# The second block's four attentions as one run of 64 steps, with masks and key bias added in PSUM

## The chip, the cores and the metric

One core of one Trainium2 chip runs the whole kernel. The metric is the device time of one execution in microseconds (us); the times are medians over several executions. Everything is float32; large products of the projections are made as three products of parts (a high part and a remainder, type fp32r).

## What is computed

Two blocks of a network over 1024 tokens of 1024 channels. The change lies in the second block, which projects its input and runs four mixers side by side, of which two are causal attentions with 4 heads of 64 channels each:

```
# forgetting attention, c = cumsum(log_sigmoid(f + bias)) per head
logits = q @ k.T * 64**-0.5 + c[query] - c[key]
logits = where(key <= query, logits, -inf);  out = softmax(logits) @ v
# stick-breaking attention
z = q @ k.T * 64**-0.5
log_rest = where(key < query, log_sigmoid(-z), 0)
between = reversed_cumsum(log_rest) - log_rest
out = where(key < query, exp(log_sigmoid(z) + between), 0) @ v
```

c[query] is the same for a whole row and falls out of the softmax; the kernel leaves it out. The mixers' outputs are gated by a sigmoid of a projection of 4096 channels, then merged, projected and followed by a feed-forward layer.

## The kernel before, in words

Engines run their own streams of instructions and wait for each other through semaphores. A part of the program between two barriers is a phase (`core.phase`, L96); at its end all engines meet and the semaphores are cleared. The second block (`second_block`, L1142) projects to a buffer in device memory (`proj2_kept`) and then runs `s5_branch`, `rwkv_branch` and `attention_branches` (L1252) in that order; `gated_branches` (L1175) follows.

**Gate tiles.** The gates' projection is 32 tiles of 128 channels, cut into 16 pieces each (two halves of 512 tokens by 8 slices of channels; a piece is three matmuls of 512 columns, L519). `GateTiles` (L494) hands pieces out: each of the three mixers calls `gates.tensor(pe, n)` wherever TensorE would wait. A half sums in one PSUM bank (bank 7, or 6 and 7 by turns where `gates.two` is set); VectorE scales it into `gate_stage` (`gates.vector`, L546), SyncE stores it and loads the weight tile after next (`gates.sync`, L557, L559, L149), and GpSimd splits the next weight tile into two parts (`gates.gpsimd`, L156, L158). Each queue is in order.

**Attentions.** After a small load (`load`, L601), a first phase makes one gate tile (16 pieces) and, for the forget bias, two 4x1024 sums and a scan on VectorE, three passes on ScalarE, and then eight products against a selector that spread the four rows over 128 partitions (L1288), which ScalarE copies out as `key_bias` (L1316). Then come four pairs of heads, forgetting first, then stick-breaking. For each pair one phase loads queries, keys and values (L1325, 1.5 MB), transposes the values on TensorE (L1332) and copies them out on ScalarE (L1339), and another runs 16 steps, one for each head and block of 128 queries. Step (n, j) has j+1 blocks of 128 keys. `causal_products` (L1349) writes TensorE's order out by hand: iteration i makes the scores of step i into one of two pairs of PSUM banks (L1362), the output of step i-3 (L1380) and the transposes of the weights of step i-2 (L1370). In the stick pairs alone 3 and 5 gate pieces by turns lie between these, 64 per pair.

A forgetting step (`forgetting_pair`, L1415) has VectorE scale the scores out of PSUM and add the key bias (L1440), add the mask on the diagonal block (L1444), take the row's largest value and negate it (L1445, L1446); ScalarE takes the exponential and its sum (L1471), VectorE the reciprocal (L1452) and the scaling (L1453). A stick step (`stick_pair`, L1475) has VectorE scale the scores out of PSUM (L1543), ScalarE make Abs, Exp and Ln (L1510 to L1512), VectorE a sum (L1527), a mask on the diagonal block (L1528), a scan (L1530), a subtraction (L1532) and another mask (L1533), and ScalarE an exponential (L1516). In both, the transposed weights are copied out of PSUM by ScalarE (L1403, helper `save_transposed`) and the output by VectorE (L1411, helper `save_output`). A score of step i+2 waits only until VectorE has copied the score of step i out of PSUM.

## Time and profile before

| | |
|---|---|
| median of 3 runs | 3998.53 us (3997.77 to 3999.42) |
| profiled execution | 3993.96 us, its span 3992.2 us |
| granted TensorE clock, mean | 0.943 |
| busy | TensorE 89%, VectorE 42%, ScalarE 19%, GpSimd 22% |
| attention stage | about 2412 to 2845 us of the span |

The profile is one execution. Windows of the span give, for each engine, the time in which it was busy; the granted clock is 1.00 at 2.4 GHz and 0.50 at 1.2 GHz. Starts in the order of time are us from the span's start. TensorE's matmuls overlap, so the distance between two starts says more than a duration. A float32 matmul appears as two records, a transpose as one.

### The profile page before, as it was taken

The page shows a single profiled execution, that of the slowest core. Times are in us where ns is not written, and L with a number is a line of the kernel's source. Part 1 is how long each engine was busy: PE and PEld are TensorE (multiplying, and loading weights), DVE is VectorE, ACT ScalarE, POOL GpSimd, SP SyncE. Part 2 cuts the span into 40 slices and gives each one's busy share as a digit, 9 for nine tenths or more (in the row PEclk, how much of TensorE's full clock was granted, in tenths as well). Part 3 has the DMA queues.
Part 4 walks back from the last instruction along what each step waited for, and adds up shares of the span by engine and source line. Part 5 has one row for each costly group of instructions (what it writes and reads, how often), then busy time and mean ns, then how long its engine had stood idle before and what let it go on. Part 6 is the DMA issues. An engine that isn't in the chain of part 4 may idle for free. (4 is left out here: it accounts for less than half of the span.)

```text
span 3992.2 us, 42576 instructions
## 1 busy us (share of the span) xinstructions
PE 3556.5 (89%) x17914; PEld 2923.2 (73%) x17914; DVE 1674.5 (42%) x2127; ACT 767.8 (19%) x1065; POOL 893.2 (22%) x513
## 2 busy tenths in 40 slices
PE   7988999998898989897877988788898799999996
PEld 6976878897687978776757975455446578888884
DVE  3225662322566251255456554656563321212134
ACT  2112331111333110000112212344320210101012
POOL 2340003234000323331124310011002133334331
PEclk9999999999999999998989997788999899999998
DMA  2120001112000133311220011011350111111111
GB/s 91 43 83 16 7 1 43 43 43 86 7 7 1 43 112 110 115 48 43 78 76 24 1 48 43 16 53 48 121 174 27 50 41 52 48 48 48 48 53 48
DMA packets 68666, 208.52 MB, mean 52 GB/s; under 512 B 10564, under 2 KB 16324, under 8 KB 68332
## 3 DMA queue, kind: packets, MB, share of 16 engines
q1 hardware_dynamic: 64012, 189.53, 14.7%
q10 hardware_dynamic: 4464, 16.25, 1.0%
q8 instruction: 143, 2.34, 0.2%
q14 instruction: 47, 0.39, 0.0%
HBM read 164.80 MB, written 40.37 MB: 51 GB/s over the span
## 5 line engine op out<-in xcount | busy, mean ns | idle before, releaser
L156 POOL CAST w_hi<-w_raw 128x1024 fp32r<-128x1024 f32 x187 | 206.7, 1105 | 2773.2 <-POOLq L104 1400.4
L158 POOL TENSOR_TENSOR w_lo<-w_raw,w_hi 128x1024 fp32r<-128x1024 f32 x187 | 511.2, 2734 | 15.0
L167 PE MATMUL psum<-h_hi,w_hi 128*128 128x512 f32 x1008 | 315.4, 394 | 35.0 <-DVE h_lo L188 29.1
L167 PE MATMUL psum<-h_lo,w_hi 128*128 128x512 f32 x1008 | 311.8, 391 | 0.0
L167 PE MATMUL psum<-h_hi,w_lo 128*128 128x512 f32 x1008 | 311.7, 390 | 0.0
L519 PE MATMUL psum<-h_hi,w_hi 128*128 128x512 f32 x512 | 217.1, 424 | 47.9 <-PEq L104 24.9
L167 PEld LDWEIGHTS psum<-h_hi,w_hi 128*128 128x128 f32 x1008 | 190.0, 189 | 79.8 <-issue 40.2
L167 PEld LDWEIGHTS psum<-h_lo,w_hi 128*128 128x128 f32 x1008 | 190.3, 189 | 39.8
L167 PEld LDWEIGHTS psum<-h_hi,w_lo 128*128 128x128 f32 x1008 | 190.1, 189 | 39.7
L519 PE MATMUL psum<-h_lo,w_hi 128*128 128x512 f32 x512 | 205.2, 401 | 0.0
L519 PE MATMUL psum<-h_hi,w_lo 128*128 128x512 f32 x512 | 204.8, 400 | 0.0
L167 PE MATMUL psum<-hn_hi,w_hi 128*128 128x348 f32 x864 | 186.6, 324 | 2.3 <-DVE hn_lo L185 2.3
L167 PE MATMUL psum<-hn_hi,w_lo 128*128 128x348 f32 x864 | 184.0, 321 | 0.0
L167 PE MATMUL psum<-hn_lo,w_hi 128*128 128x348 f32 x864 | 183.7, 321 | 0.0
L519 PEld LDWEIGHTS psum<-h_hi,w_hi 128*128 128x128 f32 x512 | 99.5, 194 | 91.2 <-issue 50.6
L167 PE MATMUL psum<-ff_lo,w_hi 128*128 128x512 f32 x512 | 157.6, 389 | 0.0
L167 PE MATMUL psum<-ff_hi,w_hi 128*128 128x512 f32 x512 | 157.6, 389 | 0.0
L167 PE MATMUL psum<-ff_hi,w_lo 128*128 128x512 f32 x512 | 157.6, 389 | 0.0
L2765 DVE TENSOR_TENSOR h_again<-psum,h_again 128x1024 f32<-128x1024 f32 x32 | 39.2, 1225 | 272.8 <-PE psum L167 272.8
L167 PEld LDWEIGHTS psum<-hn_hi,w_hi 128*128 128x128 f32 x864 | 145.8, 188 | 5.5 <-issue 3.8
L167 PEld LDWEIGHTS psum<-hn_lo,w_hi 128*128 128x128 f32 x864 | 145.7, 188 | 0.0
L167 PEld LDWEIGHTS psum<-hn_hi,w_lo 128*128 128x128 f32 x864 | 145.6, 188 | 0.0
(411 smaller groups left out, 6660.7 us busy)
## 6 DMA issues: line engine op xcount, KB each, us to landing
w_raw<-in_w_mlp SPq DMA_DIRECT2D x64, 512.0 KB, 3.6
w_raw<-in_w_in SPq DMA_DIRECT2D x36, 512.0 KB, 3.6
w_raw<-in_w_gates SPq DMA_DIRECT2D x32, 512.0 KB, 3.8
gates_kept<-gate_stage SPq DMA_DIRECT2D x64, 256.0 KB, 2.1
gates<-gates_kept SPq DMA_DIRECT2D x32, 512.0 KB, 3.6
w_raw<-in_w_out SPq DMA_DIRECT2D x24, 512.0 KB, 3.6
w_raw<-in_w_branches_in SPq DMA_DIRECT2D x23, 512.0 KB, 3.6
proj_kept<-stage ACTq DMA_DIRECT2D x23, 512.0 KB, 2.6
```

Source lines behind the costliest of these rows:

```text
L156: self.core.nc.gpsimd.tensor_copy(self.hi[:, g % 2], self.raw[:, g % 2]).then_inc(self.hi_done, 1)
L158: self.core.nc.gpsimd.tensor_tensor(self.lo[:, g % 2], self.raw[:, g % 2], self.hi[:, g % 2].bitcast(F32), ALU.subtract) \
L167: last = nc.tensor.matmul(acc[:, c, :], w[:, g % 2, k, :], x(k)[:, c * ch:(c + 1) * ch], start=(k == 0 and part == 0), stop=(k == kt - 1 a ...
L519: last = nc.tensor.matmul(self.core.psum[:, self.bank(x // KT), :], one[:, g % 2, k, :], other(k)[:, c * CH2:(c + 1) * CH2], start=(k == 0 ...
L2765: nc.vector.tensor_tensor(halves(h(m)), acc[g % 2], halves(h(m)), ALU.add) \
```

## The change

All four pairs go into one phase of 64 steps, stick-breaking pairs first. Queries are scaled by 1/8 on GpSimd when they are loaded, and queries and keys of a head stand at partitions 0 to 63, in two buffers by turns, so that a pair is loaded while an earlier one is worked on (values have one load buffer; they are transposed 8 steps ahead). The mask of the diagonal block is added by a product of the identity with the mask that sums onto the scores in PSUM. The key bias is a 65th row: ones beside the queries, the scan of the negated log-sigmoid beside the keys. ScalarE and VectorE read the scores in PSUM, and a score of step i+2 waits until the last reader of step i is done: the subtraction in a stick step (`stick_free`), the exponential in a forgetting step (`fox_exp`). Two gate pieces lie in each step, before and after the output; the first tile stands in front of the run. The largest value is taken with its sign turned in one operation. `attention_branches` takes the place of the seven functions; their removed bodies are those printed above, and the selector goes from `second_tables`:

```diff
--- before.py
+++ after.py
 def attention_branches(core, io, gates, masks, vecs, ybr):
...
-def bank_pair(core, s, n):
...
-def causal_products(core, gates, pe, qk, v, prob, probT, masks, score_free, scores_done, prob_ready,
...
-def save_transposed(core, act, i, j, probT, probT_done, probT_saved, out_done):
...
-def save_output(core, eng, i, n, j, pair, ybr, branch, out_done, out_saved):
...
-def forgetting_pair(core, gates, pair, qk, v, logits, soft, probT, key_bias, one_row, small, masks, ybr, branch):
...
-def stick_pair(core, gates, pair, qk, v, logits, soft, probT, key_bias, one_row, small, masks, ybr, branch):
...
+    gates.two = False
+    q = core.sb("queries", [P, 2, 2, T2])
+    k = core.sb("keys", [P, 2, 2, T2])
+    v_in = core.sb("values", [P, T2])
+    v = core.sb("v2", [P, 2, NQ2, P])
+    prob = core.sb("logits", [P, 3, T2])
+    rest = core.sb("rest", [P, T2])
+    small = core.sb("small2", [P, 3, 2], align=32)
+    fbias = core.sb("fbias", [HEADS2, 1], align=32)
+    nmx, total, inv = (small[:, i, :] for i in range(3))
+    f, e = gate[:, 0, :], gate[:, 1, :]
+    heads = [(1, BR_STICK, 0), (1, BR_STICK, 1), (0, BR_FOX, 0), (0, BR_FOX, 1)]
+    steps = [(p, n, j) for p in range(4) for n in range(2) for j in range(NQ2)]
+    count = len(steps)
+    def stick(i):
+        return 0 <= i < count // 2
+    def fox(i):
+        return count // 2 <= i < count
+    def width(i):
+        return (steps[i][2] + 1) * P
+    def scores(i):
+        return core.psum[:, 2 * (i % 2):2 * (i % 2) + 2, :].rearrange("p a n -> p (a n)")[:, 0:width(i)]
+    with core.phase("at_f_in", "at_q0", "at_q1", "at_k0", "at_k1", "at_v_in", "at_bias_in", "at_ones", "at_row",
+                    "at_scaled", "at_vT", "at_v", "at_f", "at_f_act", "at_scores", "sb_abs", "sb_ln", "sb_arg",
+                    "sb_free", "sb_prob", "fx_bias", "fx_exp", "fx_inv", "fx_prob", "at_T", "at_Tsaved", "at_out",
+                    "at_saved") as \
+            (block, f_in, q_in0, q_in1, k_in0, k_in1, v_in_done, bias_in, ones_set, row_set, q_scaled, vT_done,
+             v_saved, f_dve, f_act, scores_done, abs_step, ln_ready, arg_step, stick_free, stick_prob, fox_bias,
+             fox_exp, fox_inv, fox_prob, probT_done, probT_saved, out_done, out_saved):
+        q_in, k_in = (q_in0, q_in1), (k_in0, k_in1)
+            def load_pair(p):
+                kind, _, pair = heads[p]
+                m = P_ATT + 6 * kind + 3 * pair
+                if p >= 2:
+                    sp.wait_ge(out_done, 16 * (p - 1))
+                if p >= 1:
+                    sp.wait_ge(vT_done, p)
+                sp.dma_start(v_in[:], io["proj2"][m + 2]).then_inc(v_in_done, 16)
+                for n in range(2):
+                    sp.dma_start(q[0:64, p % 2, n, :], io["proj2"][m, 64 * n:64 * n + 64]).then_inc(q_in[p % 2], 16)
+                    sp.dma_start(k[0:64, p % 2, n, :], io["proj2"][m + 1, 64 * n:64 * n + 64]) \
+                        .then_inc(k_in[p % 2], 16)
+            load_pair(0)
+            sp.dma_start(f, io["proj2"][P_FORGET, 0:HEADS2, :]).then_inc(f_in, 16)
+            sp.dma_start(fbias[:], io["forget_bias"]).then_inc(f_in, 16)
+            load_pair(1)
+            sp.wait_ge(f_dve, 4)
+            for p in range(2):
+                for n in range(2):
+                    hd = 2 * p + n
+                    sp.dma_start(k[64:65, p, n, :], gate[hd:hd + 1, 0, :]).then_inc(bias_in, 16)
+            for p in range(4):
+                gates.sync(sp, 2)
+                if p < 2:
+                    load_pair(p + 2)
+            def scale_queries(p):
+                pool.wait_ge(q_in[p % 2], 32 * (p // 2 + 1))
+                nc.gpsimd.tensor_scalar(q[0:64, p % 2], q[0:64, p % 2], ATT_SCALE, None, ALU.mult) \
+                    .then_inc(q_scaled, 1)
+            nc.gpsimd.memset(one_row[:], 1.0).then_inc(ones_set, 1)
+            scale_queries(0)
+            pool.wait_ge(ones_set, 1)
+            pool.wait_ge(q_scaled, 1)
+            nc.gpsimd.memset(q[64:65], 1.0).then_inc(row_set, 1)
+            pool.wait_ge(row_set, 1)
+            scale_queries(1)
+            for p in range(4):
+                gates.gpsimd(pool, 2)
+                if p < 2:
+                    scale_queries(p + 2)
+            def value_transposes(p):
+                pe.wait_ge(v_in_done, 16 * (p + 1))
+                for t in range(NQ2):
+                    last = nc.tensor.transpose(core.psum[:, 4 + t // 4, (t % 4) * P:(t % 4 + 1) * P],
+                                               v_in[:, t * P:(t + 1) * P], masks[:, M_IDENT, :])
+                last.then_inc(vT_done, 1)
+            def score(i):
+                p, n, j = steps[i]
+                rows = slice(0, 64 if stick(i) else 65)
+                if n == 0 and j == 0:
+                    pe.wait_ge(k_in[p % 2], 32 * (p // 2 + 1))
+                    pe.wait_ge(q_scaled, p + 1)
+                    if p == 2:
+                        pe.wait_ge(row_set, 1)
+                        pe.wait_ge(bias_in, 64)
+                if stick(i - 2):
+                    pe.wait_ge(stick_free, i - 1)
+                if fox(i - 2):
+                    pe.wait_ge(fox_exp, i - 1 - count // 2)
+                for c in range((width(i) + CH2 - 1) // CH2):
+                    w = min(CH2, width(i) - c * CH2)
+                    diagonal = c == j // 4
+                    nc.tensor.matmul(core.psum[:, 2 * (i % 2) + c, 0:w], q[rows, p % 2, n, j * P:(j + 1) * P],
+                                     k[rows, p % 2, n, c * CH2:c * CH2 + w], start=True, stop=not diagonal)
+                    if diagonal:
+                        nc.tensor.matmul(core.psum[:, 2 * (i % 2) + c, w - P:w], masks[:, M_IDENT, :],
+                                         masks[:, M_NEG_FROM if stick(i) else M_NEG_AFTER, :],
+                                         start=False, stop=True).then_inc(scores_done, 1)
+            def transposes(i):
+                if stick(i):
+                    pe.wait_ge(stick_prob, i + 1)
+                else:
+                    pe.wait_ge(fox_prob, i + 1 - count // 2)
+                if i >= 1:
+                    pe.wait_ge(probT_saved, i)
+                for t in range(steps[i][2] + 1):
+                    last = nc.tensor.transpose(core.psum[:, 4 + t // 4, (t % 4) * P:(t % 4 + 1) * P],
+                                               prob[:, i % 3, t * P:(t + 1) * P], masks[:, M_IDENT, :])
+                last.then_inc(probT_done, 1)
+            def output(i):
+                p, n, j = steps[i]
+                pe.wait_ge(probT_saved, i + 1)
+                if i >= 1:
+                    pe.wait_ge(out_saved, i)
+                for t in range(j + 1):
+                    last = nc.tensor.matmul(core.psum[64 * n:64 * n + 64, 6, 0:P], v[:, p % 2, t, 64 * n:64 * n + 64],
+                                            probT[:, t, :], start=(t == 0), stop=(t == j))
+                last.then_inc(out_done, 1)
+            gates.tensor(pe, KT)
+            value_transposes(0)
+            gates.tensor(pe, KT)
+            pe.wait_ge(v_saved, 1)
+            for i in range(count + 3):
+                if i < count:
+                    score(i)
+                    gates.tensor(pe, 1)
+                    output(i - 3)
+                if i % 16 == 8 and i < count - 16:
+                    pe.wait_ge(probT_saved, i - 2)
+                    value_transposes(i // 16 + 1)
+                if i < count:
+                    gates.tensor(pe, 1)
+                if i % 16 == 8 and i < count - 16:
+                    pe.wait_ge(v_saved, i // 16 + 2)
+                if 2 <= i < count + 2:
+                    transposes(i - 2)
+            def save_values(p):
+                act.wait_ge(vT_done, p + 1)
+                nc.scalar.activation(v[:, p % 2].rearrange("p (a t) n -> p a (t n)", a=2), core.psum[:, 4:6, :],
+                                     ACT.Copy).then_inc(v_saved, 1)
+            save_values(0)
+            for i in range(count + 2):
+                if i % 16 == 8 and i < count - 16:
+                    save_values(i // 16 + 1)
+                    act.wait_ge(probT_done, i - 1)
+                    if i >= 3:
+                        act.wait_ge(out_done, i - 2)
+                    nc.scalar.activation(probT[:].rearrange("p t n -> p (t n)")[:, 0:width(i - 2)],
+                                         core.psum[:, 4:6, :].rearrange("p a n -> p (a n)")[:, 0:width(i - 2)],
+                                         ACT.Copy).then_inc(probT_saved, 1)
+                if stick(i):
+                    sp = soft[:, i % 2, 0:width(i)]
+                    act.wait_ge(scores_done, i + 1)
+                        act.wait_ge(stick_free, i - 1)
+                    step(nc.scalar.activation(sp, scores(i), ACT.Abs))
+                if fox(i):
+                    act.wait_ge(fox_bias, i + 1 - count // 2)
+                    act.wait_ge(probT_done, i - 2)
+                    nc.scalar.activation(prob[:, i % 3, 0:width(i)], scores(i), ACT.Exp, bias=nmx[:, i % 2:i % 2 + 1],
+                                         accum_out=total[:, i % 2:i % 2 + 1]).then_inc(fox_exp, 1)
+                if stick(i - 1):
+                    lg = prob[:, (i - 1) % 3, 0:width(i - 1)]
+                    act.wait_ge(stick_free, i)
+                    nc.scalar.activation(lg, lg, ACT.Exp).then_inc(stick_prob, 1)
+                if i == 0:
+                    act.wait_ge(f_dve, 1)
+                    step(nc.scalar.activation(e, f, ACT.Abs))
+                    step(nc.scalar.activation(e, e, ACT.Exp, scale=-1.0))
+                    nc.scalar.activation(e, e, ACT.Ln, bias=1.0).then_inc(f_act, 1)
+            link = chain(dve, arg_step)
+            gates.vector(dve)
+            dve.wait_ge(f_in, 32)
+            nc.vector.tensor_scalar(f, f, fbias[:, 0:1], None, ALU.add).then_inc(f_dve, 1)
+            gates.vector(dve)
+            dve.wait_ge(ones_set, 1)
+            for i in range(count + 3):
+                if i % 4 == 0 and 0 < i <= count:
+                if fox(i):
+                    b = slice(i % 2, i % 2 + 1)
+                    if i - 2 >= count // 2:
+                        dve.wait_ge(fox_exp, i - 1 - count // 2)
+                    nc.vector.reduce_max(nmx[:, b], scores(i), AX, negate=True).then_inc(fox_bias, 1)
+                if stick(i - 1):
+                    w = width(i - 1)
+                    lg, sp = prob[:, (i - 1) % 3, 0:w], soft[:, (i - 1) % 2, 0:w]
+                    dve.wait_ge(ln_ready, i)
+                    link(nc.vector.scalar_tensor_tensor(out=sp, in0=scores(i - 1), scalar=0.0, in1=sp,
+                                                        op0=ALU.max, op1=ALU.add))
+                    if i >= 2:
+                        dve.wait_ge(stick_free, i - 1)
+                    link(nc.vector.tensor_tensor_scan(rest[:, 0:w][:, ::-1], one_row[:, 0:w], sp[:, ::-1], 0.0,
+                                                      ALU.mult, ALU.add))
+                    if i >= 4:
+                        dve.wait_ge(probT_done, i - 3)
+                    nc.vector.tensor_tensor(lg, scores(i - 1), rest[:, 0:w], ALU.subtract).then_inc(stick_free, 1)
+                if fox(i - 1):
+                    b, w = slice((i - 1) % 2, (i - 1) % 2 + 1), width(i - 1)
+                    done = i - count // 2
+                    dve.wait_ge(fox_exp, done)
+                    if done >= 2:
+                        dve.wait_ge(fox_prob, done - 1)
+                    nc.vector.reciprocal(inv[:, b], total[:, b]).then_inc(fox_inv, 1)
+                    dve.wait_ge(fox_inv, done)
+                    nc.vector.tensor_scalar(prob[:, (i - 1) % 3, 0:w], prob[:, (i - 1) % 3, 0:w], inv[:, b], None,
+                                            ALU.mult).then_inc(fox_prob, 1)
+                if i == 1:
+                    dve.wait_ge(f_act, 1)
+                    nc.vector.tensor_scalar(f, f, 0.0, None, ALU.min).then_inc(f_dve, 1)
+                    dve.wait_ge(f_dve, 2)
+                    nc.vector.tensor_tensor(e, e, f, ALU.subtract).then_inc(f_dve, 1)
+                    dve.wait_ge(f_dve, 3)
+                    nc.vector.tensor_tensor_scan(f, one_row[0:HEADS2, :], e, 0.0, ALU.mult, ALU.add).then_inc(f_dve, 1)
+                    p, n, j = steps[i - 3]
+                    _, branch, pair = heads[p]
+                    rows = slice(64 * n, 64 * n + 64)
+                    dve.wait_ge(out_done, i - 2)
+                    nc.vector.tensor_copy(ybr[rows, pair + branch, j * P:(j + 1) * P],
+                                          core.psum[rows, 6, 0:P]).then_inc(out_saved, 1)
+    return {k: np.ascontiguousarray(v.astype(f32)) for k, v in dict(masks=m, s5_select=sel).items()}
```

## Rows read from the trace of the kernel before

**Rows 1.** Windows by stage: stretch, its us, busy of each engine, granted clock, DMA share, GB/s
```profile
2414.00:2442.00 28.00, 22.37 (x64) 13.65 (x64) 6.89 (x7) 9.84 (x9) 3.81 (x2) 0.80 0.14 45
2442.00:2452.00 10.00, 1.97 (x8) 1.57 (x8) 0.00 (x0) 1.02 (x1) 0.00 (x0) 0.50 0.45 158
2452.00:2475.00 23.00, 21.95 (x53) 11.48 (x54) 15.25 (x40) 7.37 (x17) 0.00 (x0) 0.50 0.00 0
2475.00:2520.00 45.00, 36.45 (x209) 25.13 (x208) 29.18 (x72) 17.51 (x32) 0.00 (x0) 0.96 0.00 1
...
2617.00:2726.00 109.00, 97.86 (x456) 67.13 (x456) 78.32 (x120) 52.74 (x81) 13.77 (x8) 0.95 0.12 39
```

**Rows 2.** Waits, attention stage: engine, line, releaser: us in total, times, longest
```profile
PE psum L1332 <- DMA qkv<-proj_kept: 32.3, 4, 8.8
```

**Rows 3.** Order of time, VectorE, end of the attentions: start, us, instruction, idle before
```profile
2844.68 0.29 DVE L1411 COPY branches<-psum 64x128 f32<-64x128 f32 x1 [3.80 <-PE psum L1380]
```

**Rows 4.** Order of time, TensorE: start of the phase; then iteration 6 of a stick pair
```profile
2417.40 0.77 PE L519 MATMUL psum<-h_hi,w_hi 128*128 128x512 f32 x1 [5.21 <-PEq L104]
...
2646.27 1.77 PE L1362 MATMUL psum<-qkv 64*128 64x512 f32 x4
2647.97 1.09 PE L1380 MATMUL psum<-probT,v 128*64 128x128 f32 x8
2648.98 0.50 PE L519 MATMUL psum<-h_hi,w_hi 128*128 128x512 f32 x1
...
2649.78 0.71 PE L1370 MATMUL psum<-masks,logits 128*128 128x128 f32 x5
2650.25 0.48 PE L519 MATMUL psum<-h_hi,w_hi 128*128 128x512 f32 x1
```

**Rows 5.** The same stretch: a ScalarE copy; a VectorE save and TensorE behind it
```profile
2650.53 0.70 ACT L1403 ACTIVATE probT<-psum 128x640 f32<-128x640 f32 x1 [1.14 <-PE psum L1370]
...
2659.82 0.28 DVE L1411 COPY branches<-psum 64x128 f32<-64x128 f32 x1
...
2660.24 1.50 PE L1380 MATMUL psum<-probT,v 128*64 128x128 f32 x12 [0.28 <-DVE branches L1411]
```

**Rows 6.** Groups by form, attention stage: line, engine, shapes, count; busy, mean ns; idle
```profile
L1530 DVE TENSOR_TENSOR_SCAN key_bias<-one_row,soft 128x1024 f32<-128x1024 f32 x4 | 9.2, 2292 | 0.1
...
L1527 DVE SCALAR_TENSOR_TENSOR soft<-logits,soft 128x512 f32<-128x512 f32 x4 | 8.6, 2139 | 0.0
L1403 ACT ACTIVATE probT<-psum 128x1024 f32<-128x1024 f32 x8 | 8.2, 1024 | 26.4 <-PE psum L1370 26.4
...
L1532 DVE TENSOR_TENSOR logits<-logits,key_bias 128x1024 f32<-128x1024 f32 x4 | 4.9, 1225 | 0.1
...
L1440 DVE SCALAR_TENSOR_TENSOR logits<-psum,key_bias 128x1024 f32<-128x1024 f32 x4 | 4.9, 1225 | 4.5 <-PE psum L1362 4.4
...
L1510 ACT ACTIVATE soft<-logits 128x1024 f32<-128x1024 f32 x4 | 4.2, 1046 | 0.0
...
L1403 ACT ACTIVATE probT<-psum 128x128 f32<-128x128 f32 x8 | 2.2, 277 | 14.5 <-PE psum L1370 14.5
...
L1530 DVE TENSOR_TENSOR_SCAN key_bias<-one_row,soft 128x128 f32<-128x128 f32 x4 | 1.7, 424 | 0.1
...
L1532 DVE TENSOR_TENSOR logits<-logits,key_bias 128x128 f32<-128x128 f32 x4 | 1.2, 293 | 0.1
```

**Rows 7.** Order of time, SyncE's queue: the first load of the attention stage
```profile
2414.16 0.27 SPq L607 DMA_DIRECT2D forget<-proj_kept  x1
```

**Rows 8.** Groups by form, GpSimd, whole span; columns as in the groups above
```profile
L158 POOL TENSOR_TENSOR w_lo<-w_raw,w_hi 128x1024 fp32r<-128x1024 f32 x187 | 511.2, 2734 | 15.0
L156 POOL CAST w_hi<-w_raw 128x1024 fp32r<-128x1024 f32 x187 | 206.7, 1105 | 2773.2 <-POOLq L104 1400.4 <-PE psum L167 1041.1 <-PE psum L519 236.1
...
L1716 POOL TENSOR_SCALAR rw_raw<-rw_raw 128x1024 f32<-128x1024 f32 x2 | 6.6, 3316 | 33.9 <-DVE rw_mixed L1683 33.8
...
L2323 POOL MEMSET s_toeplitz<- 128x2048 f32 x1 | 1.8, 1812 | 0.0
```

More of the change, by code:

```diff
@@ L1260, in attention_branches @@
     one_row = core.sb("one_row", [P, T2])
-    small = core.sb("small2", [P, 4, 2])
-    sel = core.sb("head_select", [HEADS2, HEADS2, P])
-    fbias = core.sb("fbias", [HEADS2, 1])
     gate = core.sb("forget", [HEADS2, 2, T2])
-    load(core, [(gate[:, 0, :], io["proj2"][P_FORGET, 0:HEADS2, :]), (sel[:], io["head_select"]),
-                (fbias[:], io["forget_bias"])])
-    gates.two = True
-    with core.phase("f_step_act", "f_step_dve", "c_done", "c_saved") as (block, f_act, f_dve, c_done, c_saved):
+    small = core.sb("small2", [P, 3, 2], align=32)
@@ L1306, in _ @@
-        @block.scalar
-        def _(act):
-            link = chain(act, f_act)
-            act.wait_ge(f_dve, 2)
-            f, e = gate[:, 0, :], gate[:, 1, :]
-            link(nc.scalar.activation(e, f, ACT.Abs))
-            link(nc.scalar.activation(e, e, ACT.Exp, scale=-1.0))
-            link(nc.scalar.activation(e, e, ACT.Ln, bias=1.0))
-            for n in range(HEADS2):
-                act.wait_ge(c_done, n + 1)
-                nc.scalar.activation(halves(key_bias[:, n, :]), core.psum[:, 2 + 2 * (n % 2):4 + 2 * (n % 2), :],
-                                     ACT.Copy, scale=-1.0).then_inc(c_saved, 1)
@@ L1535, in _ @@
-            for i in range(len(steps) + 3):
-                if i % 2 == 0 and 0 < i <= len(steps):
+            link = chain(dve, arg_step)
[6 more added lines that the diff above has]
+                if i % 4 == 0 and 0 < i <= count:
                     gates.vector(dve)
-                if i < len(steps):
-                    w = (steps[i][1] + 1) * P
+                if fox(i):
+                    b = slice(i % 2, i % 2 + 1)
```

206 lines of the change are left out of this document (removed).

## The prediction

> **What bounds the kernel now.** I read the windows by stage first, then the waits, then TensorE's order of time inside one step, then the groups of the ScalarE and VectorE instructions. Only the stretch from 2412 to 2845 us is touched; all else is taken as unchanged. In it TensorE never sets the pace alone: the start phase takes 28 us, and before each of the four pairs comes a stretch like the one from 2442 to 2452, 10 us in which TensorE is busy for 2 [rows 1]. There it waits for the load of queries, keys and values, 32.3 us over the four pairs [rows 2]. Behind it the granted clock stays at 0.50, the 1.2 GHz level, for 23 us in the first forgetting pair, where TensorE has only attention work; at 2475 it is back [rows 1]. A stick pair, which carries 64 pieces of gate product, lasts 109 us with TensorE busy for 98 [rows 1]. The stage ends with the last save of an output at 2844.7 + 0.3 = 2845.0 [rows 3]. A gain here counts one for one, since the next stage waits for this one, and its own first load comes only then.
>
> **Costs of one step, from TensorE's order of time.** A step has b blocks of 128 keys, b = 1 to 8. Start to start: a score of 7 blocks 1.70 us, an output of 4 blocks 1.01, one gate piece 0.80, five transposes 0.47 [rows 4]. Eight against twelve output records (4 and 6 blocks) are 1.09 and 1.50 us busy, 0.21 a block [rows 4, 5]. So: score 0.23 + 0.21b, output 0.17 + 0.21b, transposes 0.094b, piece 0.79 with its change of operands.
>
> **The change, part by part.**
> - *Mask and key bias in TensorE.* Each step gains one 128x128 product against the identity: a block of 0.21 and a change of weights of 0.1, 0.31 us. Bounds 0.2 and 0.45. The 65th row of a forgetting score adds nothing to what streams: 0; if it did, at most the 0.1 of a change per score. VectorE loses the scaling copies of the stick steps, both edits of a diagonal block, and in the forgetting steps the scale-and-add, the mask and the negation. The VectorE work that goes lies under TensorE once TensorE bounds; it counts through the chain below.
> - *Gates.* 144 pieces before and after: 16 before the first step, then two in every one of the 64 steps instead of four in each of 32. TensorE's step is then P(b) = 0.23 + 0.21b + 0.31 + 2 x 0.79 + 0.17 + 0.21b + 0.094b = 2.29 + 0.514b, over b = 1 to 8 36.8 us a head.
> - *Stick steps: a new chain.* Scores are now read where they lie, so score i+2 waits until step i's subtraction has read them. In order of time: transposes of i-2 end TensorE's iteration i; ScalarE copies them out, then Abs, Exp, Ln of i; VectorE does sum, scan, subtraction; then TensorE's whole iteration i+2 can run. ScalarE's copy goes from 277 ns at one block to 1024 at eight, 0.17 + 0.107b, and a pass over the scores is 0.02 longer (1046) [rows 6]: three are 0.57 + 0.32b. The scan is 0.157 + 0.267b and a two-input pass 0.16 + 0.133b [rows 6]: together 0.48 + 0.533b. Handovers: 0.28 from the next instruction behind the transposes (2650.25) to the copy (2650.53) [rows 4, 5], 0.14 from a VectorE end at 2660.10 to TensorE at 2660.24 [rows 5], some 0.1 for the rest. L(b) = 1.74 + 0.96b. It closes over two iterations, so a step takes (L + P)/2 = 2.01 + 0.737b, or P where that is longer (b = 1 alone, 2.80). Over b = 1 to 8: 42.7 us; four heads 171 us.
> - *Forgetting steps.* Their chain is one reduction, one exponential and the copy, at eight blocks some 1.2 + 1.1 + 1.0, and the buffer is free long before iteration i+2. They go at TensorE's P: 4 x 36.8 = 147, and 4 us for waits that I can't place.
> - *Start.* The separate load goes (first issue 2414.2, TensorE from 2417.4 [rows 4, 7]): TensorE starts at about 2414.3. Eight pieces at 0.68 are 5.5, 1.5 more for the matmuls at 1.2 GHz that the first rows after a break show, value transposes 0.9, eight pieces 5.5: first score at 2428. The four products that spread the forget row and their copies are gone (12 us, TensorE until 2440). The values' load lies under the first pieces.
> - *POOL.* In front of the first tile's split now stand the ones, the scaling of 64x2048 queries, and a 4096-element row. The nearest scaling, 128x1024, took 3.3 us, the nearest fill of 2048 1.8, cast and difference of a tile 1.1 + 2.7 [rows 8]. Queries landed at 2419, scaling 2.2 (at the cast's rate) to 6.6, row 3.6, split 3.8: 2428.6 to 2432.9, wanted at 2428.8. 0 to 4 us; I take 2.
> - *Forget bias.* The three ScalarE passes and the 4x1024 scan sit in iterations 0 and 1, partly in the wait above: 1 us (0 to 6). SP waits for the scan before the next tile's load, which is two tiles early: 0. The four bias rows are needed 32 steps later: 0.
> - *Loads of the next pair.* Those of pairs 2 and 3 wait for the 16th and 32nd output, about iteration 18 and 34, and are needed at 32 and 48: hidden under 13 steps, over 50 us. Behind that wait in SP's queue stands the load of the tile after next, 0; behind POOL's scaling stands a split due at iteration 24, 0. Without that cover each would be the 10 us of now.
> - *Values.* Three times eight transposes, a ScalarE copy of 1.0 and TensorE's wait for it in the midst of the run: 2 us each, 6 (3 to 9).
> - *End.* The last copies stand between the last outputs: 4 us more than the sum of P holds.
> - *Shared access.* A VectorE pass of 512 columns that should take 0.7 took 2.1 on average where a tile's split ran beside it [rows 6]. In a run of eight tiles and three scalings I count 3 us (0 to 14).
>
> Sum: 2428 + 2 + 171 + 151 + 1 + 6 + 4 + 3 = 2766, against 2845: 79 us less. The profiled execution took 3994.0 (span 3992.2), which gives 3915; the median of the runs is 4.6 above it, so 3920.
>
> **A rule weighed.** VectorE's pass of 1024 columns out of PSUM took 1225 ns, that out of SBUF 1225 [rows 6]: reading scores in place costs nothing extra. The Trainium skill (VectorE: DVE Perf Modes, the cycle table under the TRN2 errata) gives a PSUM source 62 cycles, 65 ns, more than an SBUF source; an estimate by that page is two such reads on each of 32 chains, 4 us, half of it per closed loop, so 2 us on the sum. The trace doesn't agree with it, and the sum goes by the trace.
>
> **Rivals.**
> - *A. TensorE bounds the stick steps too* (the two-iteration chain overlaps better than I have it). For: TensorE was busy for 98 of 109 us there. Against: today the scores leave PSUM at once. 148 in place of 171: 3897.
> - *B. More waits of POOL and VectorE on the chain.* All 14 us of shared access, 4 for the split, 5 for the forget passes, 10 for the steps' irregular widths: some 28 worse, 3948.
> - *C. The clock falls (slower than before).* With scores held in PSUM TensorE pauses in every stick step at its head; if the chip answers with 1.2 GHz, P doubles. All through, stick steps gain 32 x 4.6 / 2 = 74 us and forgetting steps 147: 4141. It ends slower than before from 79/221, 36 per cent of the run at the lower level. For: 23 us at 0.50 behind one break. Against: the breaks behind which it fell were about 10 us; from 2475 to 2520 TensorE was idle for 8.5 us of 45 in short pauses and the clock was 0.96 [rows 1]. The Trainium skill (TensorE: Matmul & The Clock Gate, the second failure mode by PSUM-queue cycling) says that such short pauses make the clock oscillate; by that rule this rival holds, and this stretch of the trace does not agree.
> - *D. The run in one piece does not hide its loads* (the head of a queue waits too long). Three loads of 10 us and their restart at the low clock, some 15 each: 3965. For it speaks only that SP, POOL and TensorE all wait in order.
>
> **How the numbers follow.** Forecast 0.71 (own range 3902 to 3940), A 0.12, B 0.09, D 0.03, C 0.05, of which 0.03 slower than before. The range takes in A with the lower bounds of mask and start, and B with some of D: 3890 to 3956. What a measurement can tell from no change is about 0.2 per cent, 8 us: faster 0.95, same 0.02, slower 0.03.
>
> **What would show it.** Right: attention from its first score to its last save about 338 us, no TensorE idle over 5 us in it, granted clock 0.98 or more; stick steps of eight blocks near 7.9 us with TensorE waiting at each score for the subtraction; forgetting steps of eight blocks near 6.4 with TensorE never waiting; ScalarE's value copies with a wait of a few us three times. Wrong: a clock under 0.9 (C), stick heads of 37 us (A), TensorE idle behind a DMA at steps 16, 32 or 48 (D), gate pieces waiting for a split (B). The forecast as a whole is wrong if the stage ends less than 40 or more than 110 us earlier.

## The result, and the profile after

The changed kernel took 3930.52 us (median of four runs, 3927.46 to 3934.08) against 3998.98 for the kernel before in the same comparison (3997.77 to 4007.15): a ratio of 0.9825, interval 0.9808 to 0.9842, some 68 us faster. The profiled execution took 3927.89 us (span 3926.1), 66.1 less than that of before; the mean granted clock went from 0.943 to 0.955. The forecast was 3920 in 3890 to 3956.

The page of the changed kernel, part 1 (busy time, share of the span, instructions). VectorE does less, as the change means; TensorE's share is up by one point.

```profile
PE 3531.9 (90%) x18026; PEld 2917.6 (74%) x18026; DVE 1606.8 (41%) x1934; ACT 753.2 (19%) x1057; POOL 922.5 (23%) x519
```

The stage is read from the store ahead of it to the end of the last save of an output. Before: 2412.94 to 2844.97, 432.0 us (its end is in [rows 3]). Now the queue of SP has the store and, 1.2 us behind it, the first load; the columns are start, duration, engine, line:

```profile
2415.40 0.32 SPq L559 DMA_DIRECT2D gates_kept<-gate_stage  x1
2416.62 0.32 SPq L1308 DMA_DIRECT2D values<-proj_kept  x1
```

and VectorE's last save:

```profile
2777.55 0.29 DVE L1515 COPY branches<-psum 64x128 f32<-64x128 f32 x1 [3.81 <-PE psum L1397]
```

So the stage takes 2777.84 - 2415.40 = 362.4 us, 69.6 less. The 2.46 by which it starts later lies in code that is the same in both. In the executions below that store lies anywhere from 2408.54 to 2422.80, so **one execution's span says little to 5 us, and the experiments are read by the length of the stage** beside their medians.

The windows of the stage, where before were the gaps and the slow clock of [rows 1]: the four stick heads in turn, and the four forgetting heads with the end. Columns: length, busy time and instructions of TensorE's matmuls, its weight loads, VectorE, ScalarE, GpSimd, then the granted clock, the DMA share and GB/s.

```profile
2431.00:2477.00 46.00, 35.32 (x140) 21.76 (x141) 30.58 (x33) 22.09 (x37) 19.77 (x8) 0.85 0.13 40
2477.00:2522.00 45.00, 39.86 (x204) 26.14 (x204) 26.22 (x34) 25.93 (x42) 1.99 (x1) 1.00 0.07 24
2522.00:2572.00 50.00, 41.66 (x195) 27.20 (x196) 29.97 (x37) 24.12 (x39) 10.17 (x4) 0.93 0.19 53
2572.00:2621.00 49.00, 42.66 (x207) 28.25 (x205) 25.60 (x33) 26.92 (x43) 3.20 (x2) 0.93 0.07 22
2621.00:2778.00 157.00, 149.84 (x849) 109.56 (x849) 68.98 (x145) 51.84 (x104) 19.17 (x9) 1.00 0.13 39
```

The forgetting heads are bound by TensorE, busy for 150 of 157 us at full clock. The stick heads are not, and three of the four have a lowered clock. What TensorE waited for in the stage (us in total, times, longest) names the rest; no load stands in it any more, where [rows 2] had 32.3 us.

```profile
PE psum L1372 <- DVE logits L1492: 24.6, 22, 3.6
PE psum L519 <- POOL w_lo L158: 7.1, 1, 7.1
PE psum L1397 <- ACT probT L1437: 3.0, 3, 1.1
PE psum L1372 <- POOL queries L1332: 2.0, 1, 2.0
PE psum L1387 <- ACT v L1427: 1.9, 3, 1.1
```

L1372 is the score, L1492 the subtraction that lets go of its PSUM buffer, L519 a gate piece, L158 GpSimd's difference in the split of a weight tile.

A second wait is gone too, which the prediction had not named: TensorE's at an output (L1380) for VectorE to save the one in front. The kernel before had 21.2 us of it over the stage, and the changed one has none. The line of before:

```profile
PE psum L1380 <- DVE branches L1411: 21.2, 17, 4.1
```

### The profile page after: what moved, and what is told of

Read it like the earlier page. It is cut to its first block and busy times, and to the rows that moved or that the text cites. A ratio compares the mean times of both kernels' runs of the same rounds, so it can differ in the third digit from the quotient of the medians.

```text
span 3926.1 us, 42521 instructions
## 1 busy us (share of the span) xinstructions
PE 3531.9 (90%) x18026; PEld 2917.6 (74%) x18026; DVE 1606.8 (41%) x1934; ACT 753.2 (19%) x1057; POOL 922.5 (23%) x519
## 3 DMA queue, kind: packets, MB, share of 16 engines
q1 hardware_dynamic: 64388, 189.54, 15.1%
## 5 line engine op out<-in xcount | busy, mean ns | idle before, releaser
L158 POOL TENSOR_TENSOR w_lo<-w_raw,w_hi 128x1024 fp32r<-128x1024 f32 x187 | 512.7, 2742 | 15.0
L519 PE MATMUL psum<-h_hi,w_hi 128*128 128x512 f32 x512 | 221.4, 432 | 52.7 <-DVE gate_stage L546 23.4
L519 PE MATMUL psum<-h_lo,w_hi 128*128 128x512 f32 x512 | 205.3, 401 | 0.0
L519 PE MATMUL psum<-h_hi,w_lo 128*128 128x512 f32 x512 | 205.2, 401 | 0.0
L519 PEld LDWEIGHTS psum<-h_hi,w_hi 128*128 128x128 f32 x512 | 99.7, 195 | 89.3 <-issue 44.8
```

The lines of the kernel that those rows point to most:

```text
L158: self.core.nc.gpsimd.tensor_tensor(self.lo[:, g % 2], self.raw[:, g % 2], self.hi[:, g % 2].bitcast(F32), ALU.subtract) \
L519: last = nc.tensor.matmul(self.core.psum[:, self.bank(x // KT), :], one[:, g % 2, k, :], other(k)[:, c * CH2:(c + 1) * CH2], start=(k == 0 ...
```

## The experiments

**The same kernel again.**

> The changed kernel once more, as the measure for the others on this chip. Both theories: 3927 to 3934 us, TensorE idle for about 7 us in front of the second gate tile, first head of 8 steps 45.8 us, third 50.1 us.

Measured: 3927.22 us (3918.80 to 3931.59), ratio 0.982 (0.9805 to 0.9835); its stage took 358.2 us, with stick heads of 47.8, 45.2, 45.1 and 46.8 where the trace above has 45.8, 45.3, 50.1 and 49.2. The last three forgetting heads agree to 0.1 us, the first took 38.6 and 40.4. A difference of 4 us in a stage is thus no finding by itself.

**Where the first head loses its time.** GpSimd's order of time in the changed kernel:

```profile
2425.54 5.37 POOL L1332 TENSOR_SCALAR queries<-queries 64x2048 f32<-64x2048 f32 x1 [7.96 <-DMA queries<-proj_kept]
2431.03 3.87 POOL L1338 MEMSET queries<- 1x4096 f32 x1
2434.97 1.03 POOL L156 CAST w_hi<-w_raw 128x1024 fp32r<-128x1024 f32 x1
2436.09 2.87 POOL L158 TENSOR_TENSOR w_lo<-w_raw,w_hi 128x1024 fp32r<-128x1024 f32 x1
2438.93 6.33 POOL L1332 TENSOR_SCALAR queries<-queries 64x2048 f32<-64x2048 f32 x1
```

The queries came at 2425.5, 6.5 us later than where I had put them. They are loaded together with the pair's keys and values, and the DMA engines were 87 per cent busy from the first issue at 2416.6 until then. [rows 1] already had 10 us for such a load, and in the run with late loads below the same five took 8.6 us. TensorE got the split at 2439.01:

```profile
2439.01 0.79 PE L519 MATMUL psum<-h_hi,w_hi 128*128 128x512 f32 x1 [7.08 <-POOL w_lo L158]
```

Meanwhile VectorE's passes over the forget row, 4x1024, ran beside GpSimd:

```profile
2425.80 5.64 DVE L1468 TENSOR_SCALAR forget<-forget,fbias 4x1024 f32<-4x1024 f32 x1 [2.54 <-DMA fbias<-in_forget_bias]
2436.78 3.24 DVE L1507 TENSOR_TENSOR forget<-forget 4x1024 f32<-4x1024 f32 x1
2440.06 5.61 DVE L1509 TENSOR_TENSOR_SCAN forget<-one_row,forget 4x1024 f32<-4x1024 f32 x1
```

The first experiment takes the scaling out of the way of the first split, with nothing else changed:

```diff
             nc.gpsimd.memset(one_row[:], 1.0).then_inc(ones_set, 1)
+            gates.gpsimd(pool)
             scale_queries(0)
...
             pool.wait_ge(row_set, 1)
-            gates.gpsimd(pool)
```

> GpSimd splits the next gate tile before it scales the first queries and writes the row of ones. Theory (GpSimd's queue at the start was costed too low): TensorE's wait of 7.1 us in front of the second gate tile goes, and with it the 9 us at 1.2 GHz behind it, worth 4 more: 8 to 12 us faster than the changed kernel. Rival (the start only shifts a wait, step 0 and 1 are bound by VectorE's forget passes, which shared access stretches): at most 4 us faster, since those passes still run beside GpSimd.

Measured: 3930.22 us, ratio 0.9837 (0.9821 to 0.9854), stage 359.2: nothing gained, as the rival had it. The wait for the split was gone, but the first head took 50.3 us. In VectorE's order of time the minimum over the forget row, a pass of 0.68 undisturbed, now lay beside the scaling, and TensorE waited at a score for VectorE instead, for 9.8 us:

```profile
2434.38 4.81 DVE L1505 TENSOR_SCALAR forget<-forget 4x1024 f32<-4x1024 f32 x1 [1.98 <-ACT forget L1461]
```
```profile
2447.05 2.07 PE L1372 MATMUL psum<-keys,queries 64*128 64x512 f32 x2 [9.77 <-DVE logits L1492]
```

The second takes the scaling off GpSimd altogether; ScalarE does it ahead of the run and in iterations 4, 24 and 40:

```diff
-                nc.gpsimd.tensor_scalar(q[0:64, p % 2], q[0:64, p % 2], ATT_SCALE, None, ALU.mult) \
-                    .then_inc(q_scaled, 1)
+                nc.scalar.activation(q[0:64, p % 2], q[0:64, p % 2], ACT.Copy, scale=ATT_SCALE).then_inc(q_scaled, 1)
```

> The four scalings of queries go from GpSimd to ScalarE, 2 us each; the row of ones is written before the first split. Theory (GpSimd's scaling of 5.4 us stretches VectorE's scan from 1.2 to 4.5 us in step 19 and the forget passes from 0.7, 1.2 and 2.3 to 5.6, 3.2 and 5.6 us): all that the kernel with the split first gains, and 3 to 8 us more, 11 to 19 us faster than the changed kernel; scans keep to 0.16 + 0.267 us a block, and the third head takes 46 us rather than 50. Rival (ScalarE is in the stick steps' chain, so its 2 us passes cost there what VectorE gains): no more than the kernel with the split first.

Measured: 3924.52 us, ratio 0.9817 (0.9802 to 0.9831), stage 355.9: far from the 11 to 19 us of the theory. The first head still took 46.9 us at a clock of 0.82; TensorE waited up to 5.58 us, again for VectorE, which had the forget passes among the first steps. What remained looked like those passes. The third head took 48.2 us where 46 was expected, with nothing of GpSimd's scaling beside it. The third keeps the second's edit, puts the forget row's loads first, and moves its passes from iterations 0 and 1 (three on ScalarE, three on VectorE) ahead of the run:

```diff
-            load_pair(0)
             sp.dma_start(f, io["proj2"][P_FORGET, 0:HEADS2, :]).then_inc(f_in, 16)
             sp.dma_start(fbias[:], io["forget_bias"]).then_inc(f_in, 16)
+            load_pair(0)
```

> On top of the scaling on ScalarE: the forget row is loaded first, and its passes on VectorE and ScalarE run under the 16 gate pieces in front of the run instead of in iterations 0 and 1. Theory (they hold up the first stick steps by 5.6 us, and the clock falls behind that wait): no TensorE wait over 3 us in the first head, granted clock 1.00 in it, that head 41 to 43 us rather than 46.9, stage 349 to 352 us rather than 356. Rival (the first head's loss is the shared start of loads and ScalarE's scaling; the passes only move into the wait for the queries): stage 355 to 358.

Measured: 3909.86 us (3906.30 to 3915.07), ratio 0.9781 (0.9765 to 0.9797), stage 344.0. The stage fell by 11.9 us and the first head by 11.5, to 35.4, both more than the theory had. And the forget passes without the other edit:

> The changed kernel with one edit: the forget row is loaded first and its passes run ahead of the 64 steps; scaling stays on GpSimd. Theory (two things hold up the first head, and each alone keeps a wait over 5 us with 1.2 GHz behind it: the forget passes on VectorE, and GpSimd's scaling and row of ones in front of the tile's split): TensorE still waits 7 us for the split, first head 43 to 46 us rather than 46 to 48, stage 355 to 360. Rival (the forget passes alone did it): first head 35 to 38 us, stage 345 to 349.

Measured: 3929.10 us, ratio 0.9824 (0.9806 to 0.9843), stage 355.8, first head 43.1, both as the theory had it. VectorE's scan of the row, now ahead of the run, is short, but a wait for the split is back, 6.04 us:

```profile
2432.49 2.28 DVE L1474 TENSOR_TENSOR_SCAN forget<-one_row,forget 4x1024 f32<-4x1024 f32 x1
```

The windows of the first head in the second, the fourth and the third of these kernels, each a line of its own trace:

```profile
2435.00:2482.00 47.00, 38.74 (x141) 23.04 (x139) 26.81 (x30) 23.60 (x38) 5.26 (x4) 0.82 0.16 49
```
```profile
2440.00:2483.00 43.00, 33.46 (x139) 20.53 (x139) 19.49 (x26) 18.78 (x34) 17.47 (x8) 0.88 0.10 35
```
```profile
2433.00:2468.00 35.00, 31.59 (x140) 19.48 (x139) 20.25 (x28) 20.38 (x35) 4.81 (x3) 1.00 0.22 66
```

With either cause left in, one wait of over 5 us remains and the clock of the head is 0.82 or 0.88; with both gone it is 1.00. Against the unchanged 358.2 the stage is 2.4 us shorter by either edit, which is within the difference of two traces of one kernel, and 14.2 by both, which is not; the ratios to the kernel before say the same. **The two causes cover each other**, and neither edit alone would have shown its worth.

**What a stick step waits for.** The theory was that a score waits two iterations for the subtraction. The experiment lets VectorE copy the scores out at once, for one more pass of its own a step; Abs and VectorE's two passes then read the copy:

```diff
+                    nc.vector.tensor_copy(prob[:, i % 3, 0:width(i)], scores(i)).then_inc(copied, 1)
...
-                    pe.wait_ge(stick_free, i - 1)
+                    pe.wait_ge(copied, i - 1)
```

> One part undone: in the stick steps VectorE copies the scores out of PSUM again, and the score of step i+2 waits for that copy alone; ScalarE and VectorE read the copy. Theory (stick steps are bound by the chain over two iterations that ends with the subtraction, and TensorE waits for it): TensorE's waits for the subtraction, 24.6 us in sum, go; a stick head of 8 steps takes 38 to 41 us rather than 45, 15 to 25 us faster than the changed kernel. Rival (VectorE's own queue of copy, sum, scan, subtraction is as long as the chain it replaces, 6.5 us at eight blocks): within 5 us either way.

Measured: 3925.35 us, ratio 0.9819 (0.9804 to 0.9834), stage 355.0. The wait at the score is gone entirely, but the heads took 44.5, 45.8, 46.2 and 45.9. The time is within 5 us of the unchanged kernel's, as the rival had it. Of what TensorE waited for, the first line is

```profile
PE psum L519 <- DVE gate_stage L546: 11.5, 5, 2.8
```

The gate pieces' accumulator (L546) is evacuated at the head of VectorE's iteration in every fourth step, and the iteration in front is late. TensorE's order of time and VectorE's around one of the five waits:

```profile
2477.79 0.48 PE L1372 MATMUL psum<-keys,queries 64*128 64x128 f32 x2
...
2481.48 0.76 PE L519 MATMUL psum<-h_hi,w_hi 128*128 128x512 f32 x1 [2.79 <-DVE gate_stage L546]
```
```profile
2478.80 1.74 DVE L1497 TENSOR_TENSOR logits<-logits,rest 128x896 f32<-128x896 f32 x1
2480.47 0.27 DVE L1520 COPY branches<-psum 64x128 f32<-64x128 f32 x1
2480.67 0.67 DVE L546 TENSOR_TENSOR gate_stage<-psum,norm_factor 128x512 f32<-128x512 f32 x1
```

The evacuation takes 0.67 us and stood behind a subtraction of seven blocks, which TensorE needs only later, for the transposes. So the same copy, with the evacuation moved up between scan and subtraction:

```diff
-                if i % 4 == 0 and 0 < i <= count:
+                if i % 4 == 0 and count // 2 < i <= count:
...
+                    if i % 4 == 3:
+                        gates.vector(dve)
```

> The changed kernel with two edits: the copy of the scores out of PSUM in the stick steps, and the gate halves taken out of PSUM between scan and subtraction. Read by heads 2 to 4 of the stick steps, which the start does not touch. Theory (the copy alone took TensorE's waits for the subtraction away, and its waits of 2.8 us for the gate bank, with the 1.2 GHz behind them, gave that back): heads of 42 to 43.5 us rather than 45.8 to 46.2, stage 344 to 350 us. Rival (the last run's short heads came from moving the scaling off GpSimd, not from the order of the gate half): heads stay over 45.

Measured: 3914.78 us (3910.19 to 3919.33), ratio 0.9789 (0.9771 to 0.9806), stage 345.0: 13.2 less than unchanged, 10.0 less than with the copy alone. Heads 43.8, 42.9, 44.6 and 41.8. The theory holds, and its rival (heads over 45 unless the scaling leaves GpSimd) doesn't. TensorE still waited 4.2 us for the evacuation. Part of the gain is the clock: in heads 2 to 4 it was at 1.2 GHz for 20.5 us with the copy alone and for 3.4 here. The third head, 0.93 before, has a full clock:

```profile
2525.00:2569.00 44.00, 38.12 (x195) 25.12 (x194) 36.33 (x43) 25.43 (x40) 9.55 (x4) 1.00 0.21 60
```

**What the mask product costs.** This kernel leaves the mask out, so its outputs are wrong; it serves for the time alone.

```diff
-                        nc.tensor.matmul(core.psum[:, 2 * (i % 2) + c, w - P:w], masks[:, M_IDENT, :],
-                                         masks[:, M_NEG_FROM if stick(i) else M_NEG_AFTER, :],
-                                         start=False, stop=True).then_inc(scores_done, 1)
+                        last.then_inc(scores_done, 1)
```

> Leaves out the 64 products that add the mask of the diagonal block, so keys behind the query count too. Read by the stage, from the store ahead of it to the last save (358 to 362 us in the changed kernel). Theory (the product costs TensorE 0.31 us a step, in full in the forgetting steps and by half in the stick steps, where the chain closes over two iterations): 15 us shorter in all, forgetting heads at 32.7 us rather than 35.2, stick heads 1.2 us shorter. Rival (it lies in TensorE's waits for the subtraction in the stick steps and costs nothing there): forgetting heads as above, stick heads as before, 10 us in all.

Measured: 3916.15 us (two runs), ratio 0.9796 (0.9772 to 0.9819), stage 345.6, 12.6 us less than 358.2. TensorE's order of time, the first score of two neighbouring forgetting heads, first after the change and then without the product:

```profile
2696.72 0.39 PE L1372 MATMUL psum<-keys,queries 65*128 65x128 f32 x2
...
2731.96 0.39 PE L1372 MATMUL psum<-keys,queries 65*128 65x128 f32 x2
```
```profile
2683.46 0.39 PE L1372 MATMUL psum<-keys,queries 65*128 65x128 f32 x2
...
2717.19 0.39 PE L1372 MATMUL psum<-keys,queries 65*128 65x128 f32 x2
```

35.24 against 33.73: 1.5 us for eight products, 0.19 each and not 0.31. The second stick head, at full clock in both kernels, took 44.3 against 45.3 and 45.2 in the two traces of the changed one: 0.12 a product, so it isn't hidden there, as the rival had it. The 12.6 us lie between theory and rival.

**What the prefetch is worth.** Loads of pairs 1 to 3 as late as they can be, still in one run, values turned at the pair's first step:

```diff
-                if p >= 2:
-                    sp.wait_ge(out_done, 16 * (p - 1))
+                if p >= 1:
+                    sp.wait_ge(out_done, 16 * p - 3)
...
-                if i % 16 == 8 and i < count - 16:
+                if i % 16 == 0 and 0 < i < count:
```

> The loads of pairs 1 to 3 are issued only when the step before the last output of the pair in front is near, and the values are transposed at the pair's first step, all within the one run. Theory (what the run saves is the restart at each pair: load, scaling, refill and low clock, 10 us at least for the load alone): each of the three changes of pair costs 12 to 20 us, 36 to 60 us on the stage, most of the change's gain. Rival (the gain is in the masks, the biases and the gate pieces, and a load of 7 us is half covered by the outputs and transposes still due): under 20 us in all.

Measured: 3973.81 us (two runs), ratio 0.994 (0.9918 to 0.9961), stage 408.3, 50.1 more than unchanged, 16.7 for each of the three pairs. TensorE's waits and, around the first change of pair, the windows:

```profile
PE psum L1370 <- POOL queries L1331: 37.9, 3, 19.0
PE psum L1370 <- issue: 14.1, 1, 14.1
```
```profile
2513.00:2523.00 10.00, 6.29 (x32) 3.82 (x30) 6.55 (x8) 7.03 (x9) 0.00 (x0) 1.00 0.00 0
2523.00:2538.00 15.00, 0.85 (x3) 0.66 (x3) 4.74 (x3) 1.80 (x2) 6.31 (x2) 0.57 0.67 158
2538.00:2543.00 5.00, 5.00 (x23) 4.08 (x24) 0.29 (x1) 0.00 (x0) 2.40 (x2) 0.59 0.01 3
```

15 us in which TensorE does three matmuls while the DMA engines are 67 per cent busy, then a start at the lower clock. So in the changed kernel the prefetch is worth 50 us. Not all of that was won from the kernel before. Each restart here also holds a scaling of the queries by GpSimd, which begins when the load has landed and which the kernel before did not have:

```profile
2531.69 5.36 POOL L1331 TENSOR_SCALAR queries<-queries 64x2048 f32<-64x2048 f32 x1 [56.63 <-DMA queries<-proj_kept]
```

Without three of these, 16 us, 34 are left. **About half of the 70 us can be put down to the cover of three of the four loads**, by this estimate; no run takes the rest apart.

**All three repairs in one.** The third kernel's edits with the copy-out and the early evacuation.

> Scaling on ScalarE, the forget passes ahead of the run, scores copied out of PSUM in the stick steps, and the gate halves taken out of PSUM ahead of VectorE's subtraction rather than behind its iteration. Theory (with the copy TensorE no longer waits for the subtraction, and what gave that back were waits of 2.8 us for the gate bank at every fourth step, behind which the clock fell to 1.2 GHz): stick heads of 40 to 43 us rather than 45 to 46, stage 335 to 345 us, about 12 to 22 us faster than the changed kernel. Rival (VectorE's queue, 33.5 us busy of 45.8 a head, bounds such steps whatever the order): heads stay at 45, stage 350 to 356.

Measured: 3897.36 us (five runs, 3890.86 to 3905.66), ratio 0.9754 (0.9738 to 0.977), where the change alone has 0.9825: 2.46 per cent off the time before instead of 1.75, some 28 us more. The stage is 330.3, stick heads 31.7, 41.9, 43.4 and 42.1. Its second head and its forgetting heads with the end:

```profile
2454.00:2496.00 42.00, 39.77 (x206) 26.35 (x206) 32.64 (x43) 26.55 (x42) 5.46 (x3) 1.00 0.07 26
2581.00:2739.00 158.00, 149.89 (x854) 109.73 (x852) 69.46 (x146) 54.41 (x106) 15.52 (x8) 1.00 0.12 39
```

The stage is shorter than the 335 to 345 us of the theory. TensorE is now busy for 39.8 of 42 us in a stick head too, which is rival A's condition, yet the head takes 42 us and not the 36.8 of bare P.

## Why the prediction was right, and where it was wrong

**The whole.** Right in direction and in the mechanism of the run: the stage is 69.6 us shorter where I had 79, and the time 10.5 above the forecast. What was to show it came out in part. From first score to last save the stage took 346.8 us and not 338, with one idle stretch of 7.1 us where none over 5 was to be, at a granted clock of 0.96 and not 0.98. Steps of eight blocks, score to score, took 7.1 to 7.4 us in the stick heads and 5.4 in the forgetting heads, not 7.9 and 6.4. A gate piece waited for a split, which was rival B's mark.

**Start.** Store to first score was to take 15.1 us (2428 - 2412.94); it took 15.65, with the queries' wait of 2.0 in it. (The four products of the working for this term are eight in the trace of before; no number hangs on it.) The row:

```profile
2431.05 0.46 PE L1372 MATMUL psum<-keys,queries 64*128 64x128 f32 x2 [2.00 <-POOL queries L1332]
```

**The first head, right by two errors.** I had 42.7 and 2 + 1 for the split and the forget passes, 45.7; it took 45.8. Undisturbed it takes 35.4. And the two start terms were worth about 10, not 3: this is the step that failed. It had the queries landed at 2419, against its own row of 10 us for a load, and they came 6.5 us later; and it had VectorE's passes at their undisturbed price, while beside GpSimd the addition took 5.64 us instead of 0.74. The wait for the split, 7.1 us, passed the upper end of 4 that I had for it.

**The four stick heads.** The 171 us for all four fit: 35.4 undisturbed and three heads of 45.2 are 171. The share of each does not, since (L + P)/2 takes a step as if its neighbours were as wide as itself. Iteration i holds the score of step i, the transposes of step i-2 and the output of step i-3, so the work of a head's wide last steps falls on the first ones of the next, which the first head does not have to bear. I worked the iterations through one after the other with the prediction's own terms, and ScalarE's exponential at a third of its three passes: this estimate gives 35.8 for the first head, 45.2 for each of the others, and for the steps of a later head 7.4, 4.9, 4.7, 4.4, 4.5, 5.9, 6.0 and 7.4 us, where the second head has 7.6, 5.2, 4.8, 4.1, 4.6, 5.6, 6.1 and 7.2.

Found were 45.3, 50.1 and 49.2 for heads 2 to 4, or 45.2, 45.1 and 46.8 in the second trace. Waiting for the subtraction is there as predicted, in 22 steps and 24.6 us. It is in the wide steps and at the changes of head:

```profile
2514.93 1.98 PE L1372 MATMUL psum<-keys,queries 64*128 64x512 f32 x4 [0.75 <-DVE logits L1492]
2522.15 0.46 PE L1372 MATMUL psum<-keys,queries 64*128 64x128 f32 x2 [1.34 <-DVE logits L1492]
...
2529.64 0.70 PE L1372 MATMUL psum<-keys,queries 64*128 64x256 f32 x2 [2.40 <-DVE logits L1492]
```

The accumulator's evacuation, which no term has, did not matter in the changed kernel: TensorE waited 0.5 us for it in the whole stage. It matters once the copy-out has removed the loop that the formula describes, which gained 3 us of stage, since TensorE next waited 11.5 us for the evacuation. The early evacuation without the copy-out was not run. With both the heads take 42 to 45 us; what holds them above 36.8 there I did not take apart.

**Shared access.** 3 us in a range of 0 to 14. In the third head the scaling started 0.25 us before a scan of VectorE:

```profile
2546.14 5.36 POOL L1332 TENSOR_SCALAR queries<-queries 64x2048 f32<-64x2048 f32 x1 [67.15 <-DMA queries<-proj_kept]
```
```profile
2546.39 4.46 DVE L1488 TENSOR_TENSOR_SCAN rest<-one_row,soft 128x512 f32<-128x512 f32 x1
```

In the second trace the scan began 0.14 us ahead of the scaling, took 1.22, and that head took 45.1 instead of 50.1:

```profile
2546.73 1.22 DVE L1488 TENSOR_TENSOR_SCAN rest<-one_row,soft 128x512 f32<-128x512 f32 x1
2546.87 6.24 POOL L1332 TENSOR_SCALAR queries<-queries 64x2048 f32<-64x2048 f32 x1 [67.48 <-DMA queries<-proj_kept]
```

Behind the stretched scan TensorE waited 3.6 us, and the clock fell. The scan's 3.2 us are thus sharing; the rest of the 5 is not shown to be, since this head took 48.2 with the scaling on ScalarE.

**Forgetting heads and end.** 147 + 4 for waits, 2 of the 6 for the values and 4 for the end: 157. Found 156.4, again by errors that cancel. A head bound by TensorE alone took 35.2 and not 36.8, of which 1.0 is the mask product at 0.19 instead of 0.31. The first head took 38.6 with the stick steps' tail. The last, which holds the end, took 45.9, so the end was worth 10.7 and not 4.

**Values.** TensorE waited 1.9 us in three waits for ScalarE's copies; with 24 transposes at 0.094 that is 4.2, in the 3 to 9. **Loads.** Hidden, and the late ones show the cover at 16.7 us a pair, near the 15 of rival D, but with GpSimd's scaling of 5.4 in it.

**Rival C** did not come, but its mechanism is there in small. The granted clock was at its lower level from 2433.3 to 2446.9, 2552.7 to 2556.2, 2566.4 to 2569.8 and 2580.1 to 2586.9, some 27 us and 7.5 per cent of the stage where the rival needed 36. Each time it fell in a wait or less than 2 us behind one, of 7.1, 3.6, 1.65 and 2.1 us; in the second trace also behind waits of 1.35 and 1.21. Yet the wait of 2.40 at 2529.64 had no such end, and the second head had a full clock through all its short ones, so the length of a wait alone does not tell. The Trainium skill (TensorE: Matmul & The Clock Gate, the second failure mode) says that short pauses for PSUM let the clock oscillate: the trace agrees for some of them, for 3.4 to 6.8 us at a time in the later heads, and not for the second head.

**The rule on PSUM sources.** The same pass of seven blocks, with the scores in PSUM (after) and in SBUF (copy-out), from the groups by form; columns: count, busy us, mean ns of one, idle before:

```profile
L1484 DVE SCALAR_TENSOR_TENSOR soft<-psum,soft 128x896 f32<-128x896 f32 x4 | 4.4, 1092 | 9.4 <-ACT soft L1447 9.4
```
```profile
L1489 DVE SCALAR_TENSOR_TENSOR soft<-logits,soft 128x896 f32<-128x896 f32 x4 | 4.4, 1093 | 0.0
```

1092 against 1093 ns. The 65 ns that the Trainium skill (VectorE: DVE Perf Modes, the cycle table) would add are not there, so leaving them out of the sum was right.

## What to carry to other kernels

When a stage is cut into runs, look first at what each restart costs, load and slow clock together: late loads made the changed kernel 50 us slower, of which by the estimate above 34 are nearer to what the kernel before had paid. When a buffer is to be held until a late reader is done, write down who is queued behind that reader, since taking the wait away only showed the next one, an evacuation of 0.67 us in the wrong place of the queue. And where two causes end at about the same time, test them together as well as apart: here each repair alone gave 2 us, no more than noise, and both gave 14. The sum of a stage can be right while its parts are not: read the parts as well.

## What the runs showed of the hardware

GpSimd's fp32 scaling of 64x2048 took 5.4 to 6.3 us, 2.6 ns and more for an element of each partition, against a cast of 128x1024 in 1.03; a fill of one partition's 4096 elements took 3.87. Beside such work VectorE's instructions stretched by far more than I had read from [rows 6]: 0.74 to 5.64 for the addition of a 4x1024 row, 0.68 to 4.81 for its minimum, 1.22 to 4.46 for a scan of 512 columns. The addition is short again, 0.74, with the scaling on ScalarE: there it kept its place in VectorE's program and no GpSimd instruction lay beside it, which shows the sharing to be the cause. What the stretched ones share is that they began inside a GpSimd instruction, by 0.26, 1.09 and 0.25 us; the scan that began 0.14 us before the scaling, and the minimum of the changed kernel, which began 0.02 before a difference of the split, kept their 1.22 and 0.68. An identical stretch of the program ended anywhere within 14 us in twelve executions, so that a gain of a few us has to be read inside its stage.
